# A three-stage encoder layer on eight cores: the last stage's weights are loaded piecewise during attention, its first norms stand beside the last output projection, the convolution is spread over the attention blocks, and its result is held twice

## The reference

```python
def encoder_layer(x, cos, sin, ...):
    x = x + 0.5 * swiglu(rms_norm(x, ffn1_norm), ffn1_w_gate, ffn1_w_up, ffn1_w_down)
    z = rms_norm(x, mix_norm) @ w_in
    b_gate, c_gate, h, q_lat, kv_lat, k_rope_raw = jnp.split(z, cuts, axis=-1)
    y_conv = short_conv_mixer(b_gate, c_gate, h, conv_w)   # B * conv3_centred(C * h), width 3, depthwise
    y_att = latent_attention(q_lat, kv_lat, k_rope_raw, cos, sin, q_norm, w_uq, kv_norm, w_ukv)
    x = x + jnp.concatenate([y_conv, y_att], axis=-1) @ w_out
    x = x + 0.5 * swiglu(rms_norm(x, ffn2_norm), ffn2_w_gate, ffn2_w_up, ffn2_w_down)
    return x
# swiglu(x) = (silu(x @ w_gate) * (x @ w_up)) @ w_down; 1024 channels, 2816 hidden
# attention: 8 heads, 64+32 dims of q and k, 64 of v, no mask; sequences of 4096 or 2048, 16 meta tokens
# in front of each; a last rms_norm with final_norm closes it
```

## Time and profile before

| | us |
|---|---|
| median of 3 runs (4775.94 to 5191.66) | 4776.9 |
| profiled execution: device time | 4784.25 |
| profiled execution: span of the slowest core (core 6) | 4782.8 |
| spans of the other seven cores | 4766.9 to 4773.4 |
| TensorE busy | 4545.1 (95%) |
| ScalarE busy | 2161.0 (45%) |
| VectorE busy | 1242.6 (26%) |
| POOL busy | 273.3 (6%) |
| attention, from its first key load that is waited for to its last PV | about 2031 to 3264.6 |
| last projection and the start of f2 | 3264.6 to 3335.4 |
| f2 from its first gate matmul on | 3335.4 to 4782.8 |

### The profile page before, as it was taken

The page is one execution under the profiler, slowest core; times in us unless marked ns, Lnnn a source line. Parts: engine busy times, 40 slices in busy tenths (PEclk is TensorE's granted clock), DMA queues, the critical chain, the costliest instruction groups (busy, mean ns, idle before and its releaser), DMA issues.

```text
span 4782.8 us, 78486 instructions; the slowest of 8 cores (4766.9 to 4782.8 us)
## 1 busy us (share of the span) xinstructions
PE 4545.1 (95%) x31256; PEld 2281.5 (48%) x31256; DVE 1242.6 (26%) x2190; ACT 2161.0 (45%) x3082; POOL 273.3 (6%) x476
## 2 busy tenths in 40 slices
PE   7999999999999999899999999985999999999999
PEld 3444444444444554455555555553444444444444
DVE  2122222222224555311111111232222222222222
ACT  2122222222224555499999999883222222222221
POOL 1000000000002122200000000001000000000000
PEclk9999999999999999999999999997999999999999
DMA  9533333333134455351111113124411111111110
GB/s 178 106 79 80 78 79 80 83 82 82 53 127 133 122 135 146 80 129 53 53 53 53 53 53 102 53 97 143 153 53 53 53 53 53 53 53 54 53 48 23
DMA packets 139047, 391.23 MB, mean 82 GB/s; under 512 B 21056, under 2 KB 44416, under 8 KB 137408
## 3 DMA queue, kind: packets, MB, share of 16 engines
q0 software_dynamic: 56512, 178.07, 15.2%
q1 hardware_dynamic: 80160, 201.46, 13.3%
q10 hardware_dynamic: 2016, 6.69, 0.4%
HBM read 318.42 MB, written 141.87 MB: 96 GB/s over the span
## 4 chain that ended last, share of the span: by engine, by line
PE 80%; ACT 8%; DVE 5%; DMA 4%; issue 3%; POOL 0%; DVEq 0%; ACTq 0%; POOLq 0%; SPq 0%
PE ps L256 18%; PE ps L259 18%; PE ps L329 16%; PE ps L1113 10%; ACT a_P L1120 6%; PE ps L656 5%; PE ps L1136 3%; PE tp L1060 3%; DMA f1wg<-ffn_w_gate 2%; PE ps L586 1%; PE tp L233 1%; PE ps L589 1%; DVE f2xn L224 1%; ACT f2stmp L346 1%; DMA f1wd<-ffn_w_down 1%
## 5 line engine op out<-in xcount | busy, mean ns | idle before, releaser
L1120 ACT ACTIVATE a_P<-ps 128x1024 bf16<-128x1024 f32 x1280 | 1185.3, 1094 | 51.7 <-PE ps L1113 49.7
L1113 PE MATMUL ps<-a_QT,a_KT 112*128 112x512 bf16 x2560 | 779.1, 386 | 47.5 <-DMA a_V<-V_d 9.2
L1136 PEld LDWEIGHTS ps<-a_V,a_P 128*128 128x128 bf16 x10240 | 489.8, 98 | 309.3 <-issue 7.7
L1136 PE MATMUL ps<-a_V,a_P 128*128 128x65 bf16 x10240 | 526.9, 194 | 0.3 <-ACT a_P L1120 0.3
L256 PE MATMUL ps<-f2xnT,f2wg 128*128 128x512 bf16 x2112 | 500.6, 380 | 1.5 <-ACT f2xnT L240 1.5
L256 PE MATMUL ps<-f1xnT,f1wg 128*128 128x512 bf16 x2112 | 500.5, 380 | 0.7 <-ACT f1xmT L240 0.7
L259 PE MATMUL ps<-f2xnT,f2wu 128*128 128x512 bf16 x2112 | 500.2, 380 | 0.0
L259 PE MATMUL ps<-f1xnT,f1wu 128*128 128x512 bf16 x2112 | 499.2, 379 | 0.0
L329 PE MATMUL ps<-f1wd,f1hT 128*128 128x512 bf16 x2112 | 469.5, 381 | 6.9 <-DMA f1wd<-ffn_w_down 5.3
L274 ACT ACTIVATE f1stmp<-ps 128x512 f32<-128x512 f32 x264 | 157.6, 597 | 700.1 <-PE ps L259 700.0
L329 PE MATMUL ps<-f2wd,f2hT 128*128 128x512 bf16 x2112 | 472.5, 383 | 0.0
(11 more groups left out here) (163 smaller groups left out, 3111.3 us busy)
## 6 DMA issues: line engine op xcount, KB each, us to landing
f1res<-xin SPq DMA_DIRECT2D x50, 512.0 KB, 3.7
f2res<-x_d SPq DMA_DIRECT2D x50, 512.0 KB, 4.2
x_d<-f1res POOLq DMA_DIRECT2D x48, 512.0 KB, 3.1
m_xin<-x_d SPq DMA_DIRECT2D x48, 512.0 KB, 3.9
a_x<-x_d SPq DMA_DIRECT2D x12, 2048.0 KB, 10.1
x_d<-a_x POOLq DMA_DIRECT2D x12, 2048.0 KB, 8.8
y<-f2res POOLq DMA_DIRECT2D x48, 512.0 KB, 3.1
f1xin<-xin SPq DMA_DIRECT2D x46, 512.0 KB, 3.8
```

The source lines that it names most:

```text
L1113: ins = nc.tensor.matmul(sbank[:, j * 512:(j + 1) * 512], lhsT=KT[h][:, kt * 128:(kt + 1) * 128], rhs=QT[qc % 2][:, h, :], start=True, sto ...
L1120: ins = nc.scalar.activation(out=Pb[:, pi % NPB, :], in_=sbank, func=AF.Exp, scale=SCALE)
L1136: ins = nc.tensor.matmul(ob[:, qs, :], lhsT=Pb[:, pi % NPB, j * 512 + qs * 128:j * 512 + (qs + 1) * 128], rhs=V[h][:, kt0 + j, :], start=( ...
```

## The change

1. **Map.** Attention's places have fixed offsets now (`KOFF`, `VOFF`, `A_...`), and f2's tiles are laid out over them (`ffn2_places`): 12 pairs' pieces of w_gate and w_up lie in the halves of the key and value places that tiles 8 to 11 don't use, 8 more in the rest of them, 2 on `uT`; w_down lies over `yc`, `yT`, `wo`, `x1`. f2's `xin` ring has one buffer instead of two. f1 keeps its map.
2. **Loads.** SP issues f2's 44 gate and up pieces (256 KB each): three after each of the eight short key loads, then one or three after each head of tile 11, the last four after the last convolution. The first four inputs of f2 (tile 0's x2) and `gB` are loaded in attention too. w_down (22 pieces) follows the last projection. POOL keeps the stores.
3. **Norms and last projection.** Norms 0 and 1 of f2 are placed ahead of the last tile's transposes, norms 2 and 3 and transposes 0 to 2 between the groups of the last projection, which uses four PSUM banks of `ps` in turn. The drain of all engines is gone.
4. **Convolution.** `conv` is cut into 16 single instructions, two blocks apart, from 12 blocks after a tile's end on, beside that tile's projection; `yc` is held twice; `load_uv` follows at 44 blocks. `o_tr` and `o_mm` start one block later, `load_x` (where a group has 7 blocks) two. The list is sorted by block number.

```diff
@@ def attn_phase
-    yc = m("yc", [128, 4, 512], BF16)
+    yc = m("yc", [128, 2, 4, 512], BF16)
...
-    def conv(tile, n):
-        if n == 0:
+    def conv(tile, n, step):
+        acc_n = acc[:, n % 2, :]
+        if n == 0 and step == 0:
             W(nc.vector, s_ul, 32 * (tile + 1))
-            W(nc.vector, s_om, 8 * tile)
...
+            W(nc.vector, s_om, 8 * (tile - 1))
...
-            W(nc.tensor, s_or, 8 * tile + i)
...
+            W(nc.tensor, s_or, 8 * tile + i - len(wob) + 1)
+        src = yc[:, tile % 2, k, :] if k < 4 else yT[:, k - 4, :]
+        bank = wob[i % len(wob)]
...
         per = 9 if tile < 7 else 7
-        steps = [(at + 3 + a, lambda a=a: o_tr(tile, a)) for a in range(4)]
+        steps = [(at + 4 + a, lambda a=a: o_tr(tile, a)) for a in range(4)]
         for i in range(8):
             for k in range(8):
-                steps.append((at + 8 + i * per + min(k, per - 1), lambda i=i, k=k: o_mm(tile, i, k)))
-        end = at + 8 + 8 * per
-        steps.append((end, lambda: load_x(tile + 1)))
+                steps.append((at + 9 + i * per + min(k, per - 1), lambda i=i, k=k: o_mm(tile, i, k)))
+        steps.append((at + 10 + 8 * per, lambda: load_x(tile + 1)))
         if tile + 1 < 12:
             for n in range(4):
-                steps.append((end + n, lambda n=n: conv(tile + 1, n)))
-            steps.append((end + 3, lambda: load_uv(tile + 2)))
+                for k in range(4):
+                    steps.append((at + 12 + 2 * (4 * n + k), lambda n=n, k=k: conv(tile + 1, n, k)))
+            steps.append((at + 44, lambda: load_uv(tile + 2)))
...
             if done[0] == 7:
                 load_kv(1, done[1])
+                next(ffn2)
+            if done[0] == 11:
+                W(nc.sync, s_pv, pvend[11 * 8 + done[1]])
+                next(ffn2)
...
     norm(*done)
-    for _, step in work + plan_out(11, 0):
-        step()
-    for e in (nc.gpsimd, nc.sync, nc.scalar, nc.vector, nc.tensor):
-        gq.drain(e)
...
+    next(ffn2)
+    wob[:] = [ps[:, i, :] for i in range(4)]
+    W(nc.tensor, s_e, nb)
+    W(nc.tensor, s_or, s_or.n)
+    for a in range(4):
+        o_tr(11, a)
+    a2["ytp"] = (s_yc, s_yc.n)
+    for i in range(8):
+        for k in range(8):
+            o_mm(11, i, k)
+        if i in (2, 4, 6):
+            next(ffn2)
@@ def ffn_phase, the part for f2
+            WT(nc.sync, a["conv"])
+            for j in (20, 21):
+                load_w("wg", j)
+                load_w("wu", j)
+            WT(nc.scalar, a["pv"])
+            WT(nc.scalar, a["conv"])
+            W(nc.vector, s_gB, 16)
+            norm(0, square(0))
+            norm(1, square(1))
+            yield
+            WT(nc.tensor, a["ytp"])
+            xpose(0)
+            norm(2, square(2))
+            yield
+            WT(nc.tensor, a["wob"])
+            xpose(1)
+            norm(3, square(3))
+            yield
+            xpose(2)
+            yield
+            xpose(3)
+            WT(nc.tensor, a["out"])
+            WT(nc.sync, a["proj"])
+            for j in range(14):
+                s_wd[j].sig(nc.sync.dma_start(out=wd[j], in_=w_d[2][:, j * 1024:(j + 1) * 1024]), 16)
+            WT(nc.sync, a["x2"][11])
...
-                    load_after(x + 2)
+                    load_after(x + R)
```

More of the change, by code:

```diff
@@ L110, in __call__, with ffn1_places @@
         return t
-def ffn_phase(nc, gq, PS, ident, epst, tag, x_src, ntile, wg_d, wu_d, wd_d, g_d, dst, gF_d=None, meta=False,
-              side=(), seam=None, handover=None):
+def ffn1_places(nc):
+    m = Map(nc, "f1")
+    m.go(0, 90112)
+    L = {}
+    wg = [m("wg%d" % i, [128, 2, 8, 128], BF16) for i in range(NJ // 2)]
+    wu = [m("wu%d" % i, [128, 2, 8, 128], BF16) for i in range(NJ // 2)]
+    L["pairs"] = list(zip(wg, wu))
+    L["wg"] = [wg[j // 2][:, j % 2, :, :] for j in range(NJ)]
+    L["wu"] = [wu[j // 2][:, j % 2, :, :] for j in range(NJ)]
+    m.go(90112, TOP - BASE)
+    L["xnT"] = [m("xnT%d" % i, [128, 8, 512], BF16) for i in range(2)]
+    xin = [m("xin%d" % i, [128, D], F32) for i in range(2)]
+    L["xn"] = m("xn", [128, 2, D], BF16)
+    L["gB"] = m("gB", [128, D], F32)
+    L["stmp"] = m("stmp", [128, 2, 512], F32)
+    wd = m("wd", [128, NJ, D], BF16)
+    L["wd_all"] = wd
+    L["wd"] = [wd[:, j, :] for j in range(NJ)]
+    L["hT"] = [m("hT%d" % j, [128, 512], BF16) for j in range(NJ)]
+    L["res"] = [m("res%d" % i, [128, D], F32) for i in range(3)]
+    L["first"] = xin + L["res"]
+    L["ring"] = xin
+    L["stat"] = m("stat", [128, 2, 4], F32)
+    L["xmT"] = m("xmT", [128, 8, NMETA], BF16)
+    L["hmT"] = m("hmT", [128, NJ, NMETA], BF16)
+    L["smt"] = m("smt", [128, 2, NMETA], F32)
+    return L
@@ L114, in ffn_phase @@
+def ffn_phase(nc, gq, PS, ident, epst, tag, L, x_src, ntile, w_d, g_d, dst, gF_d=None, meta=False, side=(),
+              seam=None, handover=None, a=None):
     tp, ps = PS
@@ L179, in ffn_phase @@
         h_end, g_end = {}, {}
[L182 removed]
         def place(x):
[L185 to L187 removed]
+            return first[x] if x < n0 else ring[(x - n0) % R]
         def load(x):
@@ L192, in load @@
             _, _, r0, rows = subs[x]
+            if a is not None:
+                for k in range(r0 // 512, (r0 + rows - 1) // 512 + 1):
+                    WT(nc.sync, a["x2"][k])
             ins = nc.sync.dma_start(out=place(x)[0:rows, :], in_=x_src[r0:r0 + rows, :])
@@ L341, in finish @@
             sub = cnt["SUB"]
-            rb = res[0:rows, sub % 3, :]
+            rb = res[sub % 3][0:rows, :]
             if final:
@@ L380, in ffn_phase @@
+        for r in range(R):
+            load_after(n0 + r)
         res_load(0)
@@ L1221, in attn_phase @@
             work.pop(0)[1]()
+        a2["x2"] = ost
+    for _, step in work:
+        step()
     norm(*done)
-    for _, step in work + plan_out(11, 0):
-        step()
-    for e in (nc.gpsimd, nc.sync, nc.scalar, nc.vector, nc.tensor):
-        gq.drain(e)
+    W(nc.sync, s_pv, s_pv.n)
+    next(ffn2)
+    a2["pv"] = (s_pv, s_pv.n)
+    a2["conv"] = (s_oc, s_oc.n)
+    a2["wob"] = (s_or, s_or.n)
+    next(ffn2)
[9 more added lines that the diff above has]
+        if i in (2, 4, 6):
+            next(ffn2)
+    a2["out"] = (s_or, s_or.n)
+    a2["proj"] = (s_om, s_om.n)
+    yield
 def build_nc():
```

254 lines of the change are left out of this document (158 added, 96 removed).

## The result

| | before | changed |
|---|---|---|
| median of this comparison (4 runs each) | 4984.28 (4775.94 to 5444.85) | 4790.06 (4725.89 to 5023.35) |
| profiled execution: device time | 4784.25 | 4728.72 |
| span of its slowest core (core 6 in both) | 4782.8 | 4727.3 |
| ratio of the undisturbed runs | | 0.990 [0.986, 0.994] |

In half of the runs of either kernel the cores of a die were granted a lower clock and took longer, which is why both medians lie far above the lowest run, and all that follows compares the other, undisturbed runs. On those the change is worth 1.0%: 4725.89 and 4728.72 instead of 4775.94 and 4776.90, where the forecast was 4730.

What follows compares the result with a forecast made beforehand. Bounds: the seam between the last PV and f2's first gate matmul, and the short tiles' attention pauses. Gains 39.8 + 3.1 + 3.6 = 46.5 us take the median from 4776.9 to 4730; range 4706 to 4746.

Steps and rivals of the forecast that it cites:

- The clock: Rival, cores running dense: clock 0.81 adds 23% to every us, 100 us give 4753, 200 eat the gain; chance 0.04.
- the seam: From the last PV's end (T) to f2's first gate matmul: 70.8 us falls to 31, -39.8.
- the pauses: Attention, three pauses around tiles 9 to 11: 25.9 us falls to 22.3, -3.6; bounds -25.9 and 0.
- it is hidden, by under 2 us: Last projection's fifth group: x1 is there at T + 19, before TensorE at T + 20.7; T is the last PV's end.
- The load of the last `x1` beside seven weight pieces: End of attention: taken as 9.4 us; full sharing with the pieces would make it 17.6 and everything 6.5 later.
- First f2 tile: Start of f2: TensorE warm and all but the last pieces landed, 79.0 to 75.95 us, -3.1.
- Rulers of 39 to 41 for tiles 9 and 10 and 36 to 37 for tile 11: Sign: us between meta-block exponentials, head 4 to head 0 taking 32.72 without a pause; VectorE's first addition waits for a DMA.
- the second chain: Between tiles: store, x1 load, first addition, as long as the convolution burst hiding it; first additions 15.8 us late in all.
- The clock term: Pauses between tiles: TensorE at 0.50 after idle times loses half of each us, +6.5 in all.
- The one-buffer ring: f2's input loads: costed at nothing, 7.9 us of cover for a landing of 3.8, at most 5.5.
- The spread pays in full: Rival, pauses: the x1 chain is faster or has slack; gain 69, 4708; chance 0.14 for gains over 56.
- Slower, by the ring: Rival, f2 norms at 33 places: landings of 9.3 us eat the gain, 11 us give 4833; chance 0.03.

Runs made afterwards that it cites:

- experiment 1: Changed kernel with x1 stored, loaded and waited for in quarters of 128 tokens; 4706.13 us in one run, 4699.6 to 4702.7 on cores 0 to 3 of the profile.
- experiment 4: Changed kernel with one PSUM bank instead of four for the last projection; 4741.25 to 4744.69 us.
- experiment 5: Changed kernel with f2's first four norms and all its transposes behind the last projection, loads still early; 4736.41 to 4739.17 us, ratio to before 0.9919.
- experiment 6: Changed kernel with all 44 gate and up pieces loaded only after the last projection; median 4727.82 us, ratio 0.9909.
- experiment 10: Changed kernel with TensorE again waiting for the last x2 store before f2's first gate matmul; 4738.94 to 4739.87 us, ratio 0.9924.
- experiment 2: Changed kernel with the convolutions of tiles 1 to 10 put back as a burst behind the last group; 4733.72 and 4735.97 us.
- experiment 3: Experiment 1's kernel (x1 in quarters) with the convolution burst of tiles 1 to 10 put back too; 4745.19 us.
- experiment 9: Changed kernel with the 896 KB load of the next queries issued 24 blocks into a tile instead of at its start; 4722.99 us in a single run.

## Why the prediction was right, and where it was not

**The number, and the step that failed.** The forecast of 4730 met the undisturbed runs (4725.89, 4728.72), and the median of all four, 4790.06, lies outside the range of 4706 to 4746. The step that failed is the one that carried the sum over to "the median of 4776.9", together with the rival "The clock", which stands in the sum with nothing, is priced for 100 and 200 us of 0.81, and was given a chance of 0.04. The median of 4776.9 came of three runs, one of which, 5191.66, showed how far a run can go; the prediction does not ask where that run came from, and takes it that such runs stay in the minority. What the runs showed in its place: two of the changed kernel's four, 4851.40 and 5023.35, had one die at a mean clock of 0.965 and 0.93, 124 and 296 us above the undisturbed ones, while the other die's cores ended at 4712.6 to 4723.1. It is not the change's doing: two of before's four, 5191.66 and 5444.85, are 415 and 668 us above its undisturbed ones, and the median of the four is 4984.28. The clock's level had been put rightly, how long it lasts and how often it comes had not. This is core 6 in the profile of experiment 1, whose cores 4 to 7 had a lower clock:

```profile
3500.00:5000.00 1500.00, 1498.19 (x5945) 628.73 (x5944) 341.41 (x491) 329.04 (x556) 23.42 (x44) 0.81 0.14 46
```

Over 1,500 us of f2 the clock is 0.81. Why it comes in some executions and not in others stays open. For the kernel itself the ratio, 0.990, is what was forecast: 4730 / 4776.9 = 0.990.

**Luck in the sum.** 46.5 us were forecast and 49 measured between undisturbed runs, but the terms were sized on one core. On core 6 they came out at -42.0, -3.0 and -5.9. On the other seven the seam gained some 39 and the pauses 7 to 13, two to three and a half times the 3.6 forecast. Their spans fell by 49 to 57 us. The number came out so close because the slowest core of the profile is the one with the longest pauses.

**The seam, -39.8 forecast, -42.0 measured.** Its parts were less exact than the sum. First group T + 7.8 (T + 9). The first groups at half clock up to T + 11.2 (T + 16.6): the clock was back after the second half-group of the first group, at 3273.10 each half takes 1.03. `x1` used from T + 18.2 (T + 19). The fifth group at T + 19.0 (T + 20.7), after a wait of 2.09 us: "it is hidden, by under 2 us" was wrong by its sign, TensorE was there first. Gate at T + 28.8 (T + 31). By experiments 4, 5, 6 and 10 the gain has four owners: four banks 17 us, the store out of the path 13, the norms beside the projection 11, the weights 1 to 4. Their sum, 42 to 45, is close to the whole, but each was undone alone and that they add up is not shown; the early loads of f2's first inputs were not undone.

**The load of the last `x1` beside seven weight pieces.** It landed in 8.7 us on core 6, no longer than the 8.3 to 9.2 of the loads between tiles, and not in the 17.6 of full sharing. Over the eight cores it was used 8.4 to 10.2 us after its issue, 9.0 on average; in experiment 6, with no pieces behind it, 7.8 to 9.1, 8.5 on average. So the pieces cost it some half a us on average, not 8. By the ring order that the prediction takes from the Trainium skill, "DMA: Bandwidth & Descriptors", section "Queues, rings and completion order", they would cost it nothing; the trace agrees but for that half us.

**First f2 tile, -3.1 forecast, -3.0 measured.** Right, but its reason was only partly the weights: experiment 6 loads them all late and loses 2.8 us there (78.84 against 76.06) and 0.8 in the seam, with no effect on the kernel that its runs can tell.

**The pauses, -3.6 forecast, -5.9 measured.** Rulers of 39 to 41 for tiles 9 and 10 and 36 to 37 for tile 11 were named, with VectorE's first addition waiting for a DMA; they were 41.22, 41.15 and 36.56. The sum itself says something else than the rulers named: 32.7 + 7.1 + 2.5 = 42.3, 41.2 and 36.9. From last addition to `x1` issue were 13.7, 13.7 and 9.6 us, where 13.9, 12.8 and 9.5 had been read, and the loads landed in 8.3 to 9.2. The size was wrong for the other cores: the store that ends the wait was read on core 6, where it took 12.4 us; on six of the other seven it took 10.4 to 11.6. Experiments 1 to 3 show the second chain that the prediction read from the issue times: remove one chain and 0 to 7 us go, remove both and the pauses are gone. The clock term holds too (0.50 at 3066 to 3069). That the store was longer at two of the three places because of the queries' load beside it is shown by experiment 9.

**Costed at nothing.** The one-buffer ring: here are TensorE's waits over f2 behind its first tile, before and changed.

```profile
PE tp L233 <- DVE f2xn L224: 36.3, 33, 1.4
```

```profile
PE tp L286 <- DVE f2xn L277: 36.0, 33, 1.2
```

They are the same. The input lands in 3.7 us at the median and 5.7 at the most, within its cover of 7.9. No square in f2 waits for a DMA. The last two pieces and w_down: no wait for them in the whole stage. The clock in the profiled execution: 1.00 through f2 on core 6, also where before had 0.84.

**The rivals.** "The spread pays in full" would have been 4708; it did not happen by itself, but is what the quarters give (4699.6 to 4706.1). "Slower, by the ring" did not show. "The clock" is answered above.
